# Half-turns in the last product, channel sums on GpSimd, and a later copy wait in attention

## The reference, cut to what matters

```
layer 0:  u = rmsnorm(h);  h += concat(mamba2_ssd(u), conformer_conv(u)) @ w_out
layer 1:  u = rmsnorm(h);  h += concat(short_conv(u), sparse_attention(u)) @ w_out
both:     u = rmsnorm(h);  h += (silu(g) * v) @ w_down,  g, v = split(causal_conv(u @ w_up))
out = rmsnorm(h) * final_norm
```

## Time and profile before

| | |
|---|---|
| median of 3 runs | 2641.39 us (2640.79 to 2642.64) |
| the profiled execution | 2642.47 us, its span 2640.8 us |
| TensorE busy | 2592.4 us (98%) |
| VectorE busy | 1733.8 us (66%) |
| ScalarE busy | 1403.6 us (53%) |
| GpSimd busy | 42.9 us (2%) |
| granted TensorE clock, mean | 0.994 |

### The profile page before, as it was taken

The page is one execution under the profiler, slowest core; times in us unless marked ns, Lnnn a source line. Parts: engine busy times, 40 slices in busy tenths (PEclk is TensorE's granted clock), DMA queues, the critical chain, the costliest instruction groups (busy, mean ns, idle before and its releaser), DMA issues.

```text
span 2640.8 us, 39151 instructions
## 1 busy us (share of the span) xinstructions
PE 2592.4 (98%) x14866; PEld 2255.0 (85%) x14866; DVE 1733.8 (66%) x2352; ACT 1403.6 (53%) x1919; POOL 42.9 (2%) x38
## 2 busy tenths in 40 slices
PE   7999999999999999999999999899999999999997
PEld 7999898888888888888888888778888888888886
DVE  4789866457755775576655666655577647764774
ACT  5578756455644554455544544654465535543553
POOL 0001200000000000000000000000000000000001
PEclk9999999999999999999999999999999999999999
DMA  6554334555555555555766566115655555555554
GB/s 206 161 190 145 112 128 156 191 196 191 189 193 192 186 186 194 191 185 176 208 200 203 160 190 191 48 49 187 212 191 191 191 192 189 185 191 194 186 177 151
DMA packets 238675, 465.67 MB, mean 176 GB/s; under 512 B 12526, under 2 KB 14174, under 8 KB 238430
## 3 DMA queue, kind: packets, MB, share of 16 engines
q1 hardware_dynamic: 237070, 461.77, 54.1%
q10 hardware_dynamic: 1488, 2.29, 0.3%
HBM read 461.94 MB, written 2.10 MB: 176 GB/s over the span
## 4 chain that ended last, share of the span: by engine, by line
PE 96%; ACT 1%; DVE 1%; issue 1%; DMA 1%; SPq 0%; ACTq 0%; DVEq 0%
PE bank L1766 33%; PE bank L1769 16%; PE bank L1803 10%; PE bank L1805 10%; PE bank L1804 10%; PE bank L2075 4%; PE bank L2076 4%; PE bank L2077 4%; PE bank L2185 1%; PE bank L2221 1%; PE bank L2120 1%; PE bank L2015 1%; PE bank L2205 0%; PE bank L1847 0%; ACT weight_head L618 0%
## 5 line engine op out<-in xcount | busy, mean ns | idle before, releaser
L1110 DVE TENSOR_TENSOR weight_tail<-weight_raw,weight_head 128x2048 fp32r<-128x2048 f32 (+1 forms) x456 | 996.6, 2186 | 800.1 <-ACT weight_head L618 798.9
L618 ACT ACTIVATE weight_head<-weight_raw 128x2048 fp32r<-128x2048 f32 (+1 forms) x456 | 832.4, 1826 | 912.2 <-DMA weight_raw<-in_ffn_w_up 318.5
L1766 PE MATMUL bank<-norm_in,weight_head 128*128 128x512 f32 x3712 | 1167.0, 396 | 0.8 <-DVE residual L1469 0.7
L1769 PEld LDWEIGHTS bank<-norm_in,weight_tail 128*128 128x128 f32 x3712 | 697.3, 188 | 164.7
L1769 PE MATMUL bank<-norm_in,weight_tail 128*128 128x256 f32 x3712 | 729.2, 278 | 0.0
L1766 PEld LDWEIGHTS bank<-norm_in,weight_head 128*128 128x128 f32 x3712 | 565.7, 189 | 2.2 <-DVE residual L1469 1.2
L1803 PE MATMUL bank<-weight_head,mixed 128*128 128x512 f32 x1088 | 424.4, 390 | 1.0 <-issue 1.0
L1805 PE MATMUL bank<-weight_head,mixed 128*128 128x512 f32 x1088 | 423.4, 389 | 0.0
L1804 PE MATMUL bank<-weight_tail,mixed 128*128 128x512 f32 x1088 | 423.3, 389 | 0.0
L2075 PE MATMUL bank<-norm_in,weight_head 128*128 128x256 f32 x896 | 260.7, 291 | 8.0 <-ACT zx L856 4.4
L2076 PE MATMUL bank<-norm_in,weight_head 128*128 128x256 f32 x896 | 255.3, 285 | 0.0
(11 more groups left out here) (293 smaller groups left out, 1588.0 us busy)
## 6 DMA issues: line engine op xcount, KB each, us to landing
weight_raw<-in_ffn_w_up SPq DMA_DIRECT2D x176, 1024.0 KB, 5.0
weight_raw<-in_ffn_w_down SPq DMA_DIRECT2D x64, 1024.0 KB, 5.1
weight_raw<-in_cd_w_in SPq DMA_DIRECT2D x64, 1024.0 KB, 5.8
weight_raw<-in_ab_w_in SPq DMA_DIRECT2D x56, 1024.0 KB, 5.0
weight_raw<-in_ab_w_out SPq DMA_DIRECT2D x32, 768.0 KB, 4.3
weight_raw<-in_ffn_w_down SPq DMA_DIRECT2D x32, 768.0 KB, 4.4
weight_raw<-in_cd_w_out SPq DMA_DIRECT2D x32, 768.0 KB, 4.4
residual<-in_x SPq DMA_DIRECT2D x4, 512.0 KB, 5.6
```

The source lines that it names most:

```text
L618: act.activation(WHEAD[:, off % RING, 0:kt * CW], WRAW[:, off % RING, 0:kt * CW], ACT.Copy)\
L1110: dve.tensor_tensor(WTAIL[:, off % RING, 0:kt * CW], WRAW[:, off % RING, 0:kt * CW], WHEAD[:, off % RING, 0:kt * CW].bitcast(F32), ALU.sub ...
L1766: pe.matmul(bank[c][:, :], head, rhs[:, u * s.kt + k, :], start=u == 0 and k == 0, stop=False)
L1769: mm = pe.matmul(bank[c][:, 0:SEQ], tail, rhs[:, u * s.kt + k, 0:SEQ], start=False, stop=u == s.units - 1 and k == s.kt - 1)
```

## The change

1. The last column group (i = 3) of `down12` is walked in half-units in the order `LAST_TURNS`: token half 0 of units 0, 1, 2, then half 1 of unit 0, half 0 of unit 3, and half 1 of units 1, 2, 3. VectorE's and ScalarE's work on half 0 is finished and stored ahead of half 1's. The root's table is loaded after group 0 by an extra square root. Half 1 is stored in four quarters (256 KB).
2. In layer 0, GpSimd adds tiles pairwise before the matmuls with ones: the conformer's eight tiles become two (one add of 128x1024, one of 128x512, into conv_acc), for the sum and for the squares, and the four tiles of squares of SSD groups 1 and 2 become one (128x512, then 128x256). TensorE sums two tiles, or one. `group_spread(1)` and `(2)` move from unit 2 to unit 3 of their groups.
3. In attention the wait for `pt_read` moves from ahead of the score products to just ahead of the compressed one.

```diff
@@ -185,6 +185,7 @@
 CONSTS = 8
+LAST_TURNS = ((0, 0), (0, 1), (0, 2), (1, 0), (0, 3), (1, 1), (1, 2), (1, 3))
 TURNS_OF_TWO = ((0, 0), (0, 1), (1, 0), (1, 1), (0, 2), (0, 3), (1, 2), (1, 3))
@@ -394,6 +395,7 @@
         tap1_mlp, mask_ready = sem("tap1_mlp"), sem("mask_ready")
+        conf_halved, ysq_halved = sem("conf_halved"), sem("ysq_halved")
         vc_cleared, prob_cleared = sem("vc_cleared"), sem("prob_cleared")
@@ -517,12 +519,17 @@
             load_mlp(1)
-            for j in range(2 * NT):
-                t, half = j // 2, ds((j % 2) * (D // 2), D // 2)
-                sp.wait_ge(store_ready if j % 2 == 0 else out_read, 2 * (t + 1))
-                sp.dma_start(out[0, t * P:(t + 1) * P, half], OST[:, t, half]).then_inc(stored, 16)
-            sp.wait_ge(stored, 16 * 2 * NT)
+            for half in range(2):
+                columns = ds(half * (D // 2), D // 2)
+                sp.wait_ge(out_read if half else store_ready, 2)
+                sp.dma_start(out[0, 0:P, columns], OST[:, 0, columns]).then_inc(stored, 16)
+            for part, ready, count in ((2, out_read, 3), (0, store_ready, 3), (3, out_read, 4), (1, store_ready, 4)):
+                columns = ds(part * CW, CW)
+                sp.wait_ge(ready, count)
+                sp.dma_start(out[0, P:2 * P, columns], OST[:, 1, columns]).then_inc(stored, 16)
+            sp.wait_ge(stored, 16 * 6)
@@ -574,6 +581,32 @@
+            def halved(out, a, b, done):
+                pool.tensor_tensor(out, a, b, ALU.add).then_inc(done, 1)
+            def conf_sums(n, first, second):
+                halved(ACC[:, :, :], first, second, conf_halved)
+                pool.wait_ge(conf_halved, 2 * n + 1)
+                halved(ACC[:, 0:2, :], ACC[:, 0:2, :], ACC[:, 2:4, :], conf_halved)
+            def group_squares_summed(g):
+                pool.wait_ge(ysq_ready, g + 1)
+                y = ZX[:, 4 * g:4 * g + 4, 0:SEQ]
+                halved(y[:, 0:2, :], y[:, 0:2, :], y[:, 2:4, :], ysq_halved)
+                pool.wait_ge(ysq_halved, 2 * g - 1)
+                halved(y[:, 0:1, :], y[:, 0:1, :], y[:, 1:2, :], ysq_halved)
+            pool.wait_ge(conf_dve, CONF_OPS)
+            conf_sums(0, CA[:, 0:4, :], CA[:, 4:8, :])
+            group_squares_summed(1)
+            pool.wait_ge(ln_sq, 1)
+            pool.wait_ge(ln_sum, 1)
+            conf_sums(1, CP[:, 0:4, 0:SEQ], CP[:, 4:8, 0:SEQ])
+            group_squares_summed(2)
             pool.wait_ge(bank_read, SPANS["out0"].tile + 4)
@@ -624,10 +657,10 @@
-            def row_squares(n, s, i):
+            def row_squares(n, s, i, rows=range(NT)):
                 part = slice(i * CW, (i + 1) * CW)
-                for t in range(NT):
+                for t in rows:
                     act.wait_ge(bank_read, s.tile + 4 * i + 2 * (t + 1))
@@ -743,14 +776,13 @@
                             row_group(s, e, i, rest(e), 2, ("mix", DT), late=i == 0)
-                        else:
+                        elif i < 3:
                             row_group(s, e, i, rest(e), 4, late=i == 0)
+                            if i == 0:
+                                act.activation(XROOT, ONES[:, 0:NT], ACT.Sqrt).then_inc(x_root, 1)
-                if norm is not None and not kts:
-                    row_squares(norm, s, i)
                 for k, kt in enumerate(kts):
@@ -1083,10 +1115,9 @@
             for t in range(NT):
+                row_squares(4, SPANS["down12"], 3, (t,))
                 act.wait_ge(var_ready, 4 + t)
                 act.activation(RSQ[:, t:t + 1], RVAR[:, t:t + 1], ACT.Sqrt).then_inc(root_ready, 1)
-            for t in range(NT):
                 act.wait_ge(rstd_ready, 4 + t)
@@ -1462,9 +1493,9 @@
-            def row_add(s, e, i, t):
-                dve.wait_ge(cols_done, e * 4 - 4 + 2 * (t + 1))
+            def row_add(s, e, i, t, left=None):
+                dve.wait_ge(cols_done, e * 4 - (2 * (NT - 1 - t) if left is None else left))
                 h = H[:, t, i * CW:(i + 1) * CW]
@@ -1572,12 +1603,10 @@
                         else:
-                            row_add(s, e, i, 0)
-                            last_factor(s, e, 0)
-                            row_add(s, e, i, 1)
-                            last_rows(0)
-                            last_factor(s, e, 1)
-                            last_rows(1)
+                            for t in range(NT):
+                                row_add(s, e, i, t, 2 * (len(LAST_TURNS) - 1 - LAST_TURNS.index((t, s.units - 1))))
+                                last_factor(s, e, t)
+                                last_rows(t)
@@ -1783,7 +1812,7 @@
-            def row_unit(s, i, u, at, lhs, banks, free, ready=None):
+            def row_unit(s, i, u, at, lhs, banks, free, ready=None, rows=range(NT)):
@@ -1822,8 +1851,12 @@
                 for i in (2, 3):
-                    row_group(s, i, lhs, (2 * (i % 2), 2 * (i % 2) + 1), (-5, -4),
-                              after=turn_behind(norm, s, i - 1) if norm is not None else None)
+                    if i == 3 and norm is None:
+                        for t, u in LAST_TURNS:
+                            row_unit(s, i, u, s.unit + i * s.units + u, lhs, (2, 3), (-5, -4), rows=(t,))
+                    else:
+                        row_group(s, i, lhs, (2 * (i % 2), 2 * (i % 2) + 1), (-5, -4),
+                                  after=turn_behind(norm, s, i - 1) if norm is not None else None)
@@ -1995,18 +2028,18 @@
                     group_spread(0)
-                if q in (12, 13) and u == 2:
+                if q in (12, 13) and u == 3:
                     group_spread(q - 11)
                 if (q, u) == (12, 0):
-                    pe.wait_ge(conf_dve, CONF_OPS)
+                    pe.wait_ge(conf_halved, 2)
                     pe.wait_ge(y_read, 2 * GROUPS)
-                    for j in range(CONF_TILES):
-                        mm = pe.matmul(bank[4][:, 0:SEQ], ONES[:, :], CA[:, j, :], start=j == 0, stop=j == CONF_TILES - 1)
+                    for j in range(2):
+                        mm = pe.matmul(bank[4][:, 0:SEQ], ONES[:, :], ACC[:, j, :], start=j == 0, stop=j == 1)
                     mm.then_inc(ln_sum, 1)
                 if (q, u) == (12, 3):
-                    pe.wait_ge(ln_sq, 1)
-                    for j in range(CONF_TILES):
-                        mm = pe.matmul(bank[5][:, 0:SEQ], ONES[:, :], CP[:, j, 0:SEQ], start=j == 0, stop=j == CONF_TILES - 1)
+                    pe.wait_ge(conf_halved, 4)
+                    for j in range(2):
+                        mm = pe.matmul(bank[5][:, 0:SEQ], ONES[:, :], ACC[:, j, :], start=j == 0, stop=j == 1)
                     mm.then_inc(ln_sum, 1)
@@ -2032,7 +2065,11 @@
-                pe.wait_ge(ysq_ready, g + 1)
+                if g in (1, 2):
+                    pe.wait_ge(ysq_halved, 2 * g)
+                else:
+                    pe.wait_ge(ysq_ready, g + 1)
+                tiles = 1 if g in (1, 2) else 4
                 sums = bank[6][:, 508:510] if g == 0 else bank[7][:, 0:NT]
@@ -2040,9 +2077,9 @@
                 for t in range(NT):
-                    for j in range(4):
+                    for j in range(tiles):
                         mm = pe.matmul(sums[:, t:t + 1], ZX[:, 4 * g + j, t * P:(t + 1) * P], ONES[:, 0:1],
-                                       start=j == 0, stop=j == 3)
+                                       start=j == 0, stop=j == tiles - 1)
                 mm.then_inc(ynorm_sum, 1)
@@ -2177,14 +2214,14 @@
                         pe.wait_ge(p_ready, 3 * (n - 1))
-                    if n >= 3:
-                        pe.wait_ge(pt_read, 2 * (n - 2))
                     qh = ZX[:, 8 + h, t * P:(t + 1) * P]
                               start=False, stop=True)
+                    if n >= 3:
+                        pe.wait_ge(pt_read, 2 * (n - 2))
                     pe.matmul(bank[2 + b][:, 0:NCMP], qh, KCR[:, g * NCMP:(g + 1) * NCMP], start=True, stop=True)\
```

## The result

The changed kernel takes 2629.14 us (median of 5 runs, 2627.58 to 2630.26) where the kernel before takes 2641.75 in the same comparison (5 runs, 2640.79 to 2643.76). The ratio is 0.995, 95% interval 0.9939 to 0.996. The forecast was 2629.6. The total hides that two of its three terms came out otherwise: attention gave 2 us more, the last product 0.9 less.

The account below looks back on a forecast made before the run. TensorE was taken to bound the kernel, working 98% of the span. Last product 5.5, channel sums 2.9 and attention 3.4 sum to 11.8 us, so 2641.39 - 11.8 = 2629.6 us; range 2624.5 to 2634.5.

Parts of the forecast that it names:

- Channel sums: Layer 0's layer-norm and group sums: TensorE does 7.7 us less; 4.4 arrive, less 1.5 for lower clock: gain 2.9 us.
- The wait at (13, 3): Layer 0, ahead of the output product: TensorE reaches this unit at 403.7, its tail is ready at 406.9, waiting 3.2 us.
- The rival by which the clock stays: Layer 0: the wait at (13, 3), shorter than 3.50 us, leaves the clock alone; 1.5 us more gain, 2628.1; chance 0.20.
- everything follows TensorE: All three places at their upper bounds, 6.0 + 7.7 + 5.3 = 19.0 us gain, so 2622.4; chance 0.04.
- Attention: Attention's weight load ahead of L2185: the copy wait goes, VectorE's scaling limits the gain; 12 x 0.28 = 3.4 us.
- Last product: Last column group and stores: half 0 finishes early, half 1's path loses the table load; span ends 5.5 us sooner.
- The weight wait: Last column group, third half-unit (0, 2): due at 2614.64, its tail ready at 2614.90, a wait of 0.3 us.
- The stream: Last stores: half of the data takes 2.6 us, flowing from 2631.7 to 2634.3; span ends at 2635.25.
- The lower bound of this term, 3.4: Last stores: the last quarter needs all the last store needed, 5.3 us, backlog included; end at 2637.4, 3.4 us less.
- GpSimd's locks delay VectorE's chain: Layer 0: adds of the squares hold VectorE's tails and group_norm(1); chain to (13, 3) 2.6 us later, 2632.2; chance 0.10.
- GpSimd holds VectorE for tens of microseconds: Layer 0's adds last 27 us; if all stood in the chain to (13, 3), 2656.6, slower; chance 0.03.
- Attention giving nothing: Attention: VectorE's scaling, already within 0.3 us, takes the place of the copy wait; no gain, 2633.0; chance 0.20.

Follow-up runs that it names:

- the shorter chain: Changed kernel with (13, 3)'s tail and group_variance(2) ahead of the Newton steps, group 2's root behind the layer norm's, the eight-tile copy later: 2625.68 us, ratio 0.9933.
- spread back: Changed kernel with group_spread(1) back behind unit (12, 2) instead of unit 3: 2629.98 us, ratio 0.9951.
- the better versions together: The shorter chain, with last-group order (0,0), (0,1), (1,0), (0,2), (1,1), (0,3), (1,2), (1,3): 2625.7 us, ratio 0.9937.

## Why the prediction was right, and where it was not

**Channel sums: predicted 2.9, measured 3.0.** Every step held. TensorE's work fell by what the pace of the old rows gave. GpSimd's adds took 2.35, 2.47 and 1.30 us and were in time. The wait at (13, 3) was 3.21 us, for 3.2. The price of the clock was charged at 1.5: from 405.84 to 413.54 there are a unit of 5.8 us and the moved spread of 0.4, so 1.5 are lost. The output product was forecast at 414.7 and started at 413.54; the difference is the 1.1 us of drift ahead of the first sum. The rival by which the clock stays (2628.1) falls with these rows. So does the one by which everything follows TensorE (2622.4), for this kernel; with another order on ScalarE, and two table loads fewer by it, the shorter chain let this part follow.

**Attention: predicted 3.4, measured 5.5.** This is the term that was mis-sized: "12 x 0.28 = 3.4 us". From the first score product to the last value product it was 1760.46 - 1668.62 = 91.84 us and is 1750.20 - 1663.82 = 86.38. The mechanism held, and VectorE's scaling is what is late next. But the 0.28 was read off one pair of items and multiplied by the number of waits, and the waits are not alike: ten are 0.28 us, one is 0.53 and one 0.73. Eight pairs of the steady part went from 5.05 to 4.70 us, which gives 2.8. They shrank by 0.35 and not by 0.28: counted from the value product ahead of it, the weight load of the turning moved up by 0.26, near the forecast, and the load behind it follows after 0.17 us instead of 0.26. Four pairs ahead of them cancel, because two of them now wait 0.44 us for VectorE's scaling. The other 2.7 us come from four items, the third to the sixth. The wait of 0.73 us stood there, in a stretch of low clock. TensorE's timeline of before, behind a wait of 5.15 us for the first exponentials:

```profile
1675.89 1.19 PE L2185 MATMUL bank<-bc,zx 128*128 128x256 f32 x2 [5.15 <-ACT prob L1072]
...
1678.99 2.05 PE L2185 MATMUL bank<-bc,zx 128*128 128x512 f32 x2 [0.73 <-ACT prob_tc L1062]
...
1683.71 1.07 PE L2185 MATMUL bank<-bc,zx 128*128 128x256 f32 x2
```

and the same items in the changed kernel:

```profile
1671.08 1.19 PE L2220 MATMUL bank<-bc,zx 128*128 128x256 f32 x2 [5.15 <-ACT prob L1104]
...
1673.24 1.91 PE L2220 MATMUL bank<-bc,zx 128*128 128x512 f32 x2
...
1677.24 0.60 PE L2220 MATMUL bank<-bc,zx 128*128 128x256 f32 x2
```

From the first of the three rows to the last it was 7.82 us and is 6.16, and the next pair took 5.61 and takes 4.53. The granted clock was 0.50 until 1685.0, 9.1 us behind the first matmul at 1675.89, in windows of 1 us of before:

```profile
1684.00:1685.00 1.00, 1.00 (x5) 0.50 0.00 0
1685.00:1686.00 1.00, 1.00 (x11) 1.00 0.00 0
```

and full from 1676.6 on in the changed kernel, 5.5 us behind the matmul at 1671.08:

```profile
1676.00:1677.00 1.00, 1.00 (x8) 0.71 0.00 0
```

With the wait's edit alone the two pairs take 10.60 us where they take 10.69 in the changed kernel and 13.43 in the one before, and attention takes 86.28 us. All twelve traces can be sorted by this edit. In the three without it (before, last product alone, sums alone) the full clock came back 8.2 to 9.3 us behind the same matmul, the two pairs take 13.0 to 13.5 us and attention 91.4 to 91.9. In the nine with it the clock came back after 3.1 to 6.3 us, the pairs take 9.8 to 11.1 and attention 85.4 to 86.8. So the edit is what brings the clock back sooner, but the moment moves by up to 3 us between traces with the same attention code: of the 5.5 us measured here, about a microsecond either way is chance. That the one wait of 0.73 us delayed the clock is what the rows suggest; no run took away that wait alone. The earlier trace rows gave a warning that I passed over: the longest of the twelve was 0.7, and I priced it as 0.28.

**Last product: predicted 5.5, measured 4.6** (13.9 - 8.6 behind TensorE's end, less 0.7 in the group). Two sizes were off. The weight wait was put at 0.3 us and is 0.45. It could have been read in the rows of before: the prediction took the group's start from the chain, 2610.56, but its first matmul stands at 2610.39, so the third half-unit was due at 2614.47 and the tail, ready at 2614.90, 0.43 us late.

```profile
2610.39 0.39 PE L1803 MATMUL bank<-weight_head,mixed 128*128 128x512 f32 x1
```

The group lost more than the wait, 0.74 us: the matmul that waited starts 0.84 us behind the one ahead of it, and the next one 0.34 us later, where the distance is 0.23. The stream was put at 2.6 us for half the data. It takes some 3.0, at 328 to 384 GB/s, in four stores of narrower rows; the run with two wide stores shows 399 to 410 again. The prediction's own sign of being wrong, stores that flow for more than 3 us behind the first quarter, was just met or just missed: the data flows from 2621.6 to 2624.6, which ends 3.8 us behind the first quarter's issue. The path from TensorE's end to the first quarter's issue is 3.67 us, for 3.65. The lower bound of this term, 3.4, was not reached, because no backlog stands ahead of half 1: half 0's data had landed by 2619.2.

**The other rivals.** That GpSimd's locks delay VectorE's chain (2632.2) falls: group_norm(1) started when the spread let it, as worked out, and the tail beside the adds at 375.79 took 2.72 us instead of 2.29 without anybody waiting for it. That GpSimd holds VectorE for tens of microseconds falls with it. But the prediction's reading of its own row, that the trace shows only part of a full block (0.8 us lost for 2.56), does not hold. What VectorE loses is what is left of GpSimd's work when the tail starts, less some 0.15 us. Before, the tail starts at 2612.35, and GpSimd's pair of products ends at 2613.29:

```profile
2610.73 2.56 POOL L599 TENSOR_TENSOR h_gained<-residual,final_gain 128x512 f32<-128x512 f32 x2 [13.74 <-DVE residual L1469]
```

That leaves 0.94 us, and the tail takes 0.79 more than its 1.76. In the changed kernel 1.01 us is left at 2601.89 and the tail takes 0.86 more; beside the adds 0.57 is left at 375.79 and it takes 0.43 more. Six more such tails, in the traces of before, of the changed kernel and of four other runs, lose what is left less 0.14 to 0.15 us. So the rows agree with VectorE waiting for GpSimd's instruction to end; the rival failed because nothing waited for the tail that was hit. Attention giving nothing (2633.0) is refuted by the run with this edit alone. With the last product's lower bound it would have been 2635.1, above the stated range, which was said to take it in.

**The sum.** 3.0 + 5.5 + 4.6 = 13.1, against 11.8 predicted, 12.6 between the medians and 13.0 between the spans without the drift of 2.1. The forecast lies 0.5 us from the time, nearer than its terms, which is luck: the errors of attention (2.1 too little) and of the last product (0.9 too much) have opposite signs, the median of before was 0.4 us higher in the comparison than the one that was subtracted from, and medians move by a microsecond.

## What to carry to other kernels

Do not price a row "so many us in so many waits" by one of the waits times their number: look at where the longest one stands, and above all whether it stands in a stretch of low clock. Here half of attention's gain came from such a stretch, and a single trace does not tell how much of it will come back in the next. When work is taken from the engine that bounds, walk the chain of the engines that feed it to its end before moving any one of its links: taking away the link that was waited for moved the wait by one unit and gained nothing, and only a chain with two table loads and one copy less on it gave the rest. A reorder that frees results earlier asks for its inputs earlier as well.

## What the hardware showed that I had not expected

- The length of a wait did not decide whether the clock fell. It fell behind waits of 3.85, 3.21 and 1.79 us and did not behind one of 1.58 (spread back). Behind a wait of 0.56 us, followed by 1.95 us of sixteen matmuls of one column each, it fell in the run with the shorter chain and stayed at 1.00 in the run of the better versions together, with the same instructions. In the changed kernel the same sixteen, with no idle time ahead, left it at 1.00 as well.
- VectorE's tail beside GpSimd's work took longer by what was left of that work at its start, less 0.15 us: 0.79 for 0.94, 0.86 for 1.01, 0.43 for 0.57.
- Four stores of 128 rows of 2 KB flow at 328 to 399 GB/s in three traces, two of 4 KB at 399 to 410 in one.
- Part of the run-to-run drift is single waits: in eight of the twelve traces a first product of an MLP waits for the residual, 0.3 to 2.3 us. It is not all of it: the run of the better versions together has no such wait, and from the output product to attention it takes 1252.79 us against the changed kernel's 1250.28.
